# A gather queue of two tables: rows of the second table issued one by one between rows of the first, instead of four after four

## What is computed

```python
s1, s2 = q[..., :half] @ keys1.T, q[..., half:] @ keys2.T      # 8 heads
v1, i1 = lax.top_k(s1, 16); v2, i2 = lax.top_k(s2, 16)
cand = v1[..., :, None] + v2[..., None, :]
sv, si = lax.top_k(cand.reshape(..., 256), 16)                 # 16 experts a head
idx = i1[si // 16] * 128 + i2[si % 16]
g = softmax(sv)
a = gelu(einsum('chkd,cd->chk', u_tab[idx], xc))               # dot with the token
out = einsum('chk,chkd->cd', g * a, v_tab[idx])                # weighted sum of rows
```

## Time and profile before

| | us |
|---|---|
| median of three executions | 2762.24 (2752.44 to 2763.79) |
| the profiled execution | 2763.79 |
| its span, first to last instruction | 2761.9 |
| POOL busy | 1489.9 (54%) |
| DVE busy | 1528.2 (55%) |
| PE busy | 1471.6 (53%) |
| ACT busy | 335.4 (12%) |
| first gather of layer 0, of layer 1 | 219.06, 2000.89 |

### The profile page before, as it was taken

One profiled execution on the slowest core, in us unless ns is written; L12 is line 12 of the kernel. 1 busy time (PEld: TensorE's weight loads), 2 busy tenths in 40 slices (PEclk: granted clock), 3 DMA queues, 4 the chain that ended last, 5 costly groups with the idle time before them and its releaser, 6 DMA issues.

```text
span 2761.9 us, 21455 instructions
## 1 busy us (share of the span) xinstructions
PE 1471.6 (53%) x6942; PEld 649.4 (24%) x6942; DVE 1528.2 (55%) x3968; ACT 335.4 (12%) x660; POOL 1489.9 (54%) x1546
## 2 busy tenths in 40 slices
PE   7887754545666565446433633369864333333334
PEld 3455311123323341112100211026541000000000
DVE  1328667658754546555656654416376676466442
ACT  1421110112201010110000000015100000000000
POOL 0005667666665546565666666610066666666664
PEclk9997976677787776667766756579877556556555
DMA  9628999999899979999999999940298999999997
GB/s 351 221 76 310 365 406 393 348 339 317 331 398 383 348 292 402 405 404 404 406 374 361 400 408 381 372 167 32 92 379 327 361 374 369 369 384 362 379 375 281
DMA packets 282573, 928.49 MB, mean 336 GB/s; under 512 B 27600, under 2 KB 28384, under 8 KB 282208
## 3 DMA queue, kind: packets, MB, share of 16 engines
q0 software_dynamic: 221184, 805.40, 76.0%
q1 hardware_dynamic: 61280, 121.73, 12.1%
HBM read 925.98 MB, written 1.05 MB: 336 GB/s over the span
## 4 chain that ended last, share of the span: by engine, by line
PE 22%; DVE 20%; POOL 17%; issue 15%; DMA 14%; another core or an unknown queue 9%; ACT 2%; SPq 0%; POOLq 0%; DVEq 0%; ACTq 0%
POOL RING L609 17%; DVE RING L693 10%; DMA RING<-in_p_v,IDV 10%; PE acc L1165 5%; PE wk L1365 5%; DMA RING<-in_p_u,IDX 4%; PE wk L1227 3%; PE wk L1350 2%; PE wk L1151 1%; DVE TI L682 1%; PE wk L1194 1%; PE wk L1309 1%; DVE TV L679 1%; DVE OHR L943 1%
## 5 line engine op out<-in xcount | busy, mean ns | idle before, releaser
L693 DVE SCALAR_TENSOR_TENSOR RING<-RING,acc 128x1024 f32<-128x1024 f32 x768 | 911.3, 1219 | 447.9 <-DMA RING<-in_p_u,IDX 310.5
L1165 PE MATMUL acc<-RING,ST 128*32 128x512 f32 x3072 | 633.5, 955 | 971.1 <-DMA RING<-in_p_v,IDV 744.5
L609 POOL DMA_INDIRECT RING<-in_p_u,IDX x768 | 748.7, 975 | 682.8 <-DVE WG L957 403.5
L609 POOL DMA_INDIRECT RING<-in_p_v,IDV x768 | 739.6, 963 | 570.6 <-PE acc L1165 209.0
L1165 PEld LDWEIGHTS acc<-RING,ST 128*32 128x32 f32 x3072 | 123.2, 148 | 1385.5 <-issue 1360.2
L1365 PE MATMUL wk<-HT,WR 128*128 128x256 f32 x768 | 202.3, 422 | 54.6 <-issue 34.2
L1365 PEld LDWEIGHTS wk<-HT,WR 128*128 128x128 f32 x768 | 162.5, 214 | 98.8 <-issue 72.8
L1397 PE MATMUL wk<-SELW,WE 128*128 128x512 f32 x96 | 78.2, 907 | 94.4 <-DVE WE L714 77.2
L1227 PE MATMUL wk<-WR,HT 128*128 128x512 f32 x256 | 117.1, 614 | 6.1 <-DMA WR<-in_o_w_in 3.8
L679 DVE MAX8 TV<-SCR 128x8 f32<-128x128 f32 x192 | 41.9, 281 | 98.8 <-ACT SCR L1115 56.6
L1124 ACT ACTIVATE GA<-A 128x16 f32<-128x16 f32 x48 | 10.3, 215 | 695.4 <-issue 497.9
(11 more groups left out here) (177 smaller groups left out, 1541.5 us busy)
## 6 DMA issues: line engine op xcount, KB each, us to landing
WR<-in_ada_w SPq DMA_DIRECT2D x31, 1024.0 KB
WR<-in_p_w_q SPq DMA_DIRECT2D x24, 1024.0 KB
RING<-in_ada_w SPq DMA_DIRECT2D x17, 1024.0 KB, 13.6
WR<-in_o_w_in SPq DMA_DIRECT2D x14, 1024.0 KB
RING<-in_p_u,IDX POOLq DMA_INDIRECT x768
RING<-in_p_v,IDV POOLq DMA_INDIRECT x768
WR<-in_e_w_in SPq DMA_DIRECT2D x8, 1024.0 KB
WR<-in_e_w_out SPq DMA_DIRECT2D x7, 1024.0 KB
```

Source lines behind the costliest of these rows:

```text
L609: pool.indirect_dma_start(out=ring[:, n % NU, :], out_offset=None, in_=tables[table], in_offset=bass.IndirectOffsetOnAxis(ap=rows, axis=0) ...
L693: nc.vector.scalar_tensor_tensor(out=U[:, s % NU, :], in0=U[:, s % NU, :], scalar=1.0, in1=acc[:, 1, :], op0=ALU.mult, op1=ALU.mult, accum ...
L1165: ins = nc.tensor.matmul(acc[32 * g:32 * g + 32, 0, hf * 512:hf * 512 + 512], ST[:, c % 2, s, :], V[:, s % NV, hf * 512:hf * 512 + 512], s ...
```

## The change

Within a step, the gathers from the two tables alternate slot by slot instead of standing four after four. The waits in front of each gather, the buffers, the number of gathers and all other engines' programs stay the same. In the first chunk of a layer (only `p_u`) and behind the last one (only `p_v`) the order stays as it was.

```diff
                     for s_ in range(4 * q, 4 * q + 4):
                         gather_u(c, s_)
-                    if c > 32 * l:
-                        for s_ in range(4 * q, 4 * q + 4):
+                        if c > 32 * l:
                             gather_v(c - 1, s_)
```

## The result

The changed kernel took 2774.97 us (median of 9, 2766.17 to 2795.08), the kernel before on the same chip 2756.69 us (median of 9, 2752.44 to 2763.79): a ratio of 1.0076, 95% interval 1.0055 to 1.0097. The change costs 18 us, 0.8%. The forecast was 2883 us, 121 more than before. The sign was right, the size almost seven times too large.

The account below looks back on a forecast made before the run. POOL's gather pace, in a ring of waits with the sums, was taken to bound part of the kernel. 131 - 10 = 121 us on the profiled 2763.79 gave 2885, forecast as 2883 us against the median; range 2755 to 2970.

Parts of the forecast that it names:

- 35 waits: Waits on a step's first v, 17 in layer 0 and 18 in layer 1, each growing 3.74 us: 131 us.
- first class: Waits before a step's first v where POOL's pace rules: the last v is summed within 8 us of issue.
- late release: In layer 1, v buffers released 9.5 us late; held to end with the next sums or a PE event, not POOL.
- 3.74 us a wait: Behind a wait on v0, v0 to v3 take six places instead of three, so the last v leaves 3.74 us later.
- The u later: u1 to u3 issued one to three places later, DVE's last dot up to 3.74 us later: 0, or 172 uncovered.
- The second class: 26 first-v waits where the transfers rule, nearly all near 405 GB/s; backlog keeps transfers busy: 0, at most 97 us.
- Attention: Eight first-v waits at 590 to 730 us; v lands some 17 us before its use: 0, at most 30 us.
- -10 us for DVE's waits: POOL's own waits for DVE, 65.1 us in all, shrink where POOL comes later: 10 us back, between 0 and 65.
- The transfers hide it: Rival: gathers alone can draw only 362 GB/s and POOL's waits mirror a full queue; 2762 us, chance 0.11.
- Faster: Rival: four gathers in a row of one table cause the late release, alternating ends it; 2690 to 2650 us, chance 0.09.
- Slower still: Rival: the late release becomes more frequent, or its small forms are common, among 85 non-waiting steps; above 2963 us, chance 0.11.

Follow-up runs that it names:

- e10: The alternating order in layer 1 alone, full rows, against the kernel before: 2605.16 us, ratio 1.0016.
- e9: The alternating order in layer 0 alone, full rows, against the kernel before: 2611.61 us, ratio 1.0040.
- e8: The changed order with half rows (512 of 1024 words of each `p_v` row gathered), against the kernel before: 2483.82 us, ratio 0.9554.
- e3: Order u0 v0 v1 v2 v3 u1 u2 u3, full rows, against the kernel before: 2603.27 us, ratio 1.0010.
- e1: Order v0 v1 v2 v3 u0 u1 u2 u3, full rows, against the kernel before: 2614.93 us, ratio 1.0051.
- e15: Half rows of `p_v` with order v0 v1 v2 v3 u0 u1 u2 u3, upper level, against the kernel before: 2750.73 us, ratio 0.9920.
- e16: Half rows of `p_v` with order u0 v0 v1 v2 v3 u1 u2 u3, upper level, against the kernel before: 2738.38 us, ratio 0.9883.
- e7: Half rows of `p_v` (512 of 1024 words gathered) in the order of before, against the kernel before: 2443.24 us, ratio 0.9397.

## Why the prediction was wrong

The step that failed is "Cost: 35 waits in the first class x 3.74 = 131 us", and in it the sentence that v0 "would have its turn at 2298.34 and still start near 2306.26". Only six of the 35 waits are ended by PE's sums; the other 29 are the late release, and it did not stay where it was.

- **3.74 us a wait.** Right in size where PE's sums end the wait and the transfers leave room: with half rows 3 places cost 40.6 us, some eleven times 3.74, and 2 and 4 places cost about in proportion. Wrong for the late release. In 29 of the 35 waits POOL starts 3.1 to 10.7 us behind the end of the sums, in the other six 0.25 us. In layer 1, where 17 of my 18 lie, the wait before v0 went from 4.1 to 3.0 us in the median and not to about 8. The prediction held that the release hangs on PE and not on POOL; at v0's earlier turn it came earlier.
- **35 waits.** Wrong. I took a last v that lands within 8 us as proof that POOL's pace rules. It only shows that the queue is short at that moment. Of the 67 us for layer 1, 3.5 came at the lower level (e10), and 11.5 in the two profiled executions at the upper one. In layer 0, 10 us came of 64 at the lower level (e9), and 0.3 at the upper one. The waits that cost at the lower level are those of a v buffer that PE holds behind a long piece of its own work, as in the earlier trace rows; in layer 0 of e8 I count eleven waits of a first v of over 2.5 us, and in the 16 us ahead of ten of them most of PE's work was other than sums. At full rows the change costs 15.0 us in place of 40.6; I take it that the rest comes out of the transfers' stock, which no run shows by itself.
- **The u later: 0.** Right (e3, 1.5 us), with e1's 13 us, where all four u are later, left open.
- **The second class: 0**, and 1050 to 1400 us at about 405 GB/s. Right: 401. **Attention: 0.** Roughly; 450 to 750 us even has four gathers more than before.
- **-10 us for DVE's waits.** Wrong in sign: 65.1 us before, 74.9 after.
- **The rivals.** "The transfers hide it" is the nearest, 2762 against 2775, and at the lower level it holds in most places, though at 398 to 409 GB/s and not at the 362 from which I argued. At the upper level it isn't the bytes, as e15 and e16 show. "Faster" got half its mechanism: the waits of over 4 us do become fewer in layer 1, ten before and four after, but smaller ones take their time and a little more. "Slower still" rested on a wrong count: I find 87 steps whose last v is summed within 8 us, not 120, so 52 of them did not wait, not 85.

What stays open: what makes the counts late at the upper level, and so what the 18 us there are made of. That six waits at 3.74 would be 22 us is no proof of it: five of the six lie in layer 0, and the profiled executions differ in layer 1. The gather of 2306.26 starts 5.43 us after the start of POOL's last one, and many that waited long in before and e15 do after a like time; together with the earlier release of the change this looks as if the counts came once POOL stood still, but no run tried that. No order tried beats the one before.

## What to carry to other kernels

A wait on the engine that issues transfers is a cost only where the queue behind it can run dry; quick landing does not prove that. Count work per window (gathers per us) before pricing waits: where the same rate comes out of a window whatever the order, a wait is a remainder and not a term of a sum. To see what an order is worth by itself, take bytes away first; then the price shows (here, at the lower level, 1.25 us for each place fewer between the last gather of a step and the first reuse of its buffers, at each wait behind long work of the other engine). And look at what ends a wait before you hold its end fixed: where the engine named had long been done, the end can move with the change.

## What the runs showed of the hardware

- The same kernel had two levels, 2600 to 2602 us and 2757 to 2776, which all kernels of a round shared; each round ran on another chip. In layer 1 a gather of 512 KB took 1.29 us at the lower level (402 in 520 us) and 1.42 at the upper one (24 in 34.1 us), at like granted clocks of TensorE (0.60, and 0.60 and 0.61).
- A release reached POOL 0.26 us after the end of the sums at the lower level (853 to 858 us of e7). At the upper one it came 12.7 us after it in e15 (2302.64), 9.5 us in before and 6.5 us in the change; there the semaphore's counts themselves come late in the trace, and POOL still starts 0.26 us behind them.
- Between two indirect gathers POOL shows 0.30 us of idle time; two memsets of 128x1 with their semaphores fit into it without moving the next gather.
